# The opening of a fused conformer, attention and MoE kernel: scale's half of the modulation first, the first block's shift as a bias, x's norm with tokens on partitions

## The reference, cut to what matters

```python
def first_block(x, c, ...):
    sc_l = jax.nn.silu(c)                                   # (1, 1024)
    mod_l = (sc_l @ w_mod[i] + b_mod[i])[:, None, :]        # (1, 1, 6144)
    sh1_l, s1_l, g1_l, sh2_l, s2_l, g2_l = jnp.split(mod_l, 6, axis=-1)
    hl = rms_norm(xl, norm1_g[i]) * (1.0 + s1_l) + sh1_l
    yl = conformer_conv(hl, rows, *conv_p)
    xl = xl + g1_l * yl
    ...

def conformer_conv(h, n_seg, w_pw1, b_pw1, w_dw, ...):
    u = h @ w_pw1 + b_pw1                                   # (512, 2048)
    a, gate = jnp.split(u, 2, axis=-1)
    u = a * jax.nn.sigmoid(gate)
    u = dwconv(...)                                         # width 31, in 8 segments of 64 tokens
    ...
```

## Time and profile before

| | |
|---|---|
| Time, median of 3 runs | 2239.32 us (2237.25 to 2240.61) |
| The profiled execution: its own time | 2237.78 us |
| Its span, first to last instruction | 2236.0 us |
| Mean granted TensorE clock | 0.984 |
| Busy: PE, DVE, ACT, POOL | 2166.1 (97%), 989.0 (44%), 396.8 (18%), 69.2 (3%) us |
| First matmul of pw1(0) / first of conv(0) | 36.86 us / 66.80 us from the span's start |

### The profile page before, as it was taken

The page is one execution under the profiler, slowest core; times in us unless marked ns, Lnnn a source line. Parts: engine busy times, 40 slices in busy tenths (PEclk is TensorE's granted clock), DMA queues, the critical chain, the costliest instruction groups (busy, mean ns, idle before and its releaser), DMA issues.

```text
span 2236.0 us, 25125 instructions
## 1 busy us (share of the span) xinstructions
PE 2166.1 (97%) x10252; PEld 1314.6 (59%) x10252; DVE 989.0 (44%) x1435; ACT 396.8 (18%) x783; POOL 69.2 (3%) x89
## 2 busy tenths in 40 slices
PE   7999999999999999998999999999999899999998
PEld 3343488878886777865544444436888544444443
DVE  3883297788855644843122222125555322222222
ACT  3214222002113122842100000002000200000000
POOL 1100100000012000000000000001000000000000
PEclk9999999999999999998999999999999899999999
DMA  9416334577650112032899999996112599999996
GB/s 351 156 44 227 112 131 171 200 252 264 225 207 14 63 39 89 1 151 113 335 428 429 429 427 430 428 425 245 67 76 92 210 423 429 428 428 429 429 428 272
DMA packets 106460, 564.24 MB, mean 252 GB/s; under 512 B 8840, under 2 KB 17550, under 8 KB 78734
## 3 DMA queue, kind: packets, MB, share of 16 engines
q1 hardware_dynamic: 105952, 563.03, 62.6%
q10 hardware_dynamic: 430, 0.13, 0.0%
HBM read 561.04 MB, written 2.10 MB: 252 GB/s over the span
## 4 chain that ended last, share of the span: by engine, by line
PE 84%; DMA 12%; DVE 3%; issue 1%; ACT 1%; SPq 0%; DVEq 0%; ACTq 0%
PE psum L1629 24%; PE psum L2072 16%; PE psum L2058 8%; PE psum L1368 8%; DMA ring<-in_moe_w_down_dram 6%; PE psum L2151 5%; PE psum L1777 4%; PE psum L2108 3%; PE psum L1801 3%; PE psum L1958 2%; PE psum L1934 2%; DMA ring<-in_moe_w_up_dram 2%; PE psum L1909 2%; PE psum L1576 2%; DMA ring<-in_conv_w_pw_dram 1%; DMA ring<-in_mlp_w_dram 1%
## 5 line engine op out<-in xcount | busy, mean ns | idle before, releaser
L2072 PE MATMUL psum<-ring,arena 128*64 128x512 f32 x2048 | 444.8, 593 | 5.8 <-DMA ring<-in_moe_w_up_dram 5.8
L2072 PEld LDWEIGHTS psum<-ring,arena 128*64 128x64 f32 x2048 | 145.0, 137 | 302.3 <-issue 286.0
L2058 PE MATMUL psum<-ring,arena 128*64 128x512 f32 x768 | 224.9, 594 | 2.3 <-DMA ring<-in_moe_w_down_dram 2.0
L2943 DVE TENSOR_TENSOR arena<-psum,arena 128x512 f32<-128x512 f32 x32 | 33.8, 1058 | 410.9 <-PE psum L2072 410.9
L1368 PE MATMUL psum<-hT,ring 128*128 128x512 f32 x416 | 182.1, 597 | 3.7 <-DMA ring<-in_conv_w_pw_dram 3.7
L1629 PE MATMUL psum<-ring 128*128 128x256 f32 x640 | 142.9, 380 | 4.8 <-DVE rstd L2526 4.7
L1368 PEld LDWEIGHTS psum<-hT,ring 128*128 128x128 f32 x416 | 79.3, 192 | 103.2 <-issue 97.7
L1629 PE MATMUL psum<-hT,ring 128*128 128x256 f32 x608 | 138.6, 384 | 0.8 <-ACT hT L891 0.8
L1629 PEld LDWEIGHTS psum<-ring 128*128 128x128 f32 x640 | 121.0, 190 | 24.6 <-issue 8.4
L2108 PEld LDWEIGHTS psum<-arena 128*128 128x128 f32 x1024 | 121.2, 198 | 14.0 <-issue 14.0
L2108 PE MATMUL psum<-arena 128*128 128x128 f32 x1024 | 125.4, 283 | 2.5 <-DVE arena L2970 2.5
(11 more groups left out here) (406 smaller groups left out, 2557.9 us busy)
## 6 DMA issues: line engine op xcount, KB each, us to landing
ring<-in_moe_w_gate_dram SPq DMA_DIRECT2D x64, 2048.0 KB, 19.1
ring<-in_moe_w_up_dram SPq DMA_DIRECT2D x64, 2048.0 KB, 16.4
ring<-in_moe_w_down_dram SPq DMA_DIRECT2D x44, 2048.0 KB, 20.7
ring<-in_ada_w_dram SPq DMA_DIRECT2D x24, 2048.0 KB, 9.0
ring<-in_mlp_w_dram SPq DMA_DIRECT2D x16, 2048.0 KB, 8.6
...
```

Of the source, the lines that this page charges most:

```text
L2058: ins = pe.matmul(psum[64 * e:64 * e + 64, bank + nh, :], src[:, 4 * h + k, 64 * e:64 * e + 64], w[:, k, nh * N:(nh + 1) * N], start=h == ...
L2072: ins = pe.matmul(psum[64 * nh:64 * nh + 64, bank + e, :], src[:, 4 * h + k, 64 * e:64 * e + 64], w[:, k, nh * N:(nh + 1) * N], start=h == ...
```

## The change

Weights. SP's list starts with scale's columns of w_mod alone (`B_SCALE`, two blocks of 4 k by 1024 columns), then pw1's first block, then shift's columns (`B_MOD[0]`, two blocks), then as before. Rows of w_mod are now laid so that partition p holds rows 8p to 8p+7 (`(p k)`), for rounds 0 to 2. `K` moves to ACT's DMA queue, ahead of the vectors, with c loaded once more as `c_own` in the same layout.

Norm. ACT squares `x_tok`, tokens on partitions, with the sum along the row (four 128x1024 instructions), takes the root of 128x4 and DVE the reciprocal of 128x4; four matmuls spread it over the partitions into PSUM (`x_wide`). `norm_stat(NORM1)` and the 128x512 root and reciprocal go.

Modulation. PE multiplies c with scale's first block between x's sixth and seventh tile, with the second after the vectors' turn, copies and turns the rows (`turn_rows(1, ...)`); DVE makes the gain from them and scales x from PSUM's rstd. pw1(0) starts on `hT` without the shift. Then PE multiplies c with shift's half, turns it (`mod_turn(0)`), runs pw1(1)'s first tile, `shift_bias` (the shift times pw1's first block: 16 matmuls of 32x256), pw1(1)'s second tile, and turns the result (`turn_rows(2, ...)`). DVE adds it to b_pw1 as `pw1_bias`, with which ACT takes out the tiles of pw1(0) and pw1(1). ACT adds the shift to `hT` after that, for pw1(2) on.

The rest of the diff renames semaphores and the counts that they reach.

```diff
-        return [add(mods[a][256 * b:256 * b + 256, 2048 * part:2048 * part + 2048].rearrange("(k p) n -> p k n", p=P),
+        return [add(mods[a][:, 2048 * part:2048 * part + 2048].rearrange("(p k) n -> p k n", k=DT)[:, 2 * b:2 * b + 2, :],
                     ("mod_row", rnd + 1)) for b in range(4)]
-    B_MOD = {0: add_mod(0)}
+    B_MOD = {}
+    B_SCALE = [add(mods[0][:, D:2 * D].rearrange("(p k) n -> p k n", k=DT)[:, 4 * b:4 * b + 4, :], ("row_raw", 1))
+               for b in range(2)]
@@ -158,6 +160,9 @@
     for b in range(4):
         B_PW1[b] = add([pw1_rows[:, :, 256 * b + D * (1 - m):256 * b + D * (1 - m) + 256] for m in range(2)],
                        ("tile_done", T_PW1[2 * b + 1] + 2))
+        if b == 0:
+            B_MOD[0] = [add(mods[0][:, 0:D].rearrange("(p k) n -> p k n", k=DT)[:, 4 * m:4 * m + 4, :], ("mod_row", 1))
+                        for m in range(2)]
...
-            squares(NORM1, xT, emptied(T_X))
-            root(NORM1)
+            act.wait_ge(S["x_in"], 32)
+            act.activation(cpad[:, :, 0], c_own[:, :], ACT.Silu).then_inc(S["c_own"], 1)
+            for t in range(NT):
+                ins = act.activation(carve(arena, 6656 + D * t, D), x_tok[:, t, :], ACT.Square,
+                                     accum_out=n_tok[:, 0, t:t + 1])
+            ins.then_inc(S["x_ms"], 1)
+            act.wait_ge(S["x_ms"], 1)
+            act.activation(n_tok[:, 0, :], n_tok[:, 0, :], ACT.Sqrt, scale=1.0 / D, bias=eps[:, 0:1]).then_inc(S["x_rms"], 1)
+            act.wait_ge(S["row_raw"], 1)
+            act.activation(mod_rows[:, :], psum[:, MISC, :], ACT.Copy).then_inc(S["row_sb"], 1)
             act.wait_ge(*emptied(T_V)(0))
-            act.activation(cpad[:, :, 0:3], vecT[:, 0:24].rearrange("p (i k) -> p k i", i=3), ACT.Silu)\
+            act.activation(cpad[:, :, 1:3], vecT[:, 8:24].rearrange("p (i k) -> p k i", i=2), ACT.Silu)\
                 .then_inc(S["c_silu"], 1)
             mod_row(0)
             mod_turned(0)
-            act.wait_ge(S["mod_ready"], 1)
-            shift(NORM1, hT, modv[:, 0, 0:8])
+            act.wait_ge(S["row_raw"], 2)
+            act.activation(mod_rows[:, 0:H], psum[:, STAT, 0:H], ACT.Copy).then_inc(S["row_sb"], 1)
...
                     col = COL["b_pw1"] + (8 if m == 0 else 0) + j
+                    bias = vecT[:, col:col + 1]
+                    if j < 2:
+                        act.wait_ge(S["pw1_bias"], 1)
+                        bias = pw1_bias[:, 2 * m + j:2 * m + j + 1]
                     act.activation(dst[:, j % 2, :], psum[:, t % 6, :], ACT.Sigmoid if m == 0 else ACT.Identity,
-                                   bias=vecT[:, col:col + 1]).then_inc(FREE["act"], 1)
+                                   bias=bias).then_inc(FREE["act"], 1)
+                if m == 0:
+                    act.wait_ge(S["mod_ready"], 1)
+                    shift(NORM1, hT, modv[:, 0, 0:8])
                 conv_out(2 * m)
                 if m == 3:
...
+            def half_gemv(bs):
+
+                for k in range(4 * bs[0], 4 * bs[-1] + 4):
+                    w = arrived(pe, (B_SCALE, B_MOD[0])[len(bs) - 1][k // 4])
+                    for h in range(2):
+                        q = 2 * (k % 2) + h
+                        ins = pe.matmul(psum[32 * q:32 * q + 32, MISC, :], cpad[:, k, :], w[:, k % 4, h * N:(h + 1) * N],
+                                        start=k < 2, stop=k >= DT - 2, skip_group_check=True)
+                return ins
+
+            def turn_rows(n, js):
+
+                pe.wait_ge(S["row_sb"], n)
+                bank = (MISC, STAT)[n - 1]
+                for j in js:
+                    ins = pe.transpose(psum[:, bank, j * P:(j + 1) * P], mod_rows[:, j * P:(j + 1) * P], ident)
+                ins.then_inc(S["row_turned"], 1)
+
+            def shift_bias():
+
+                pe.wait_ge(S["mod_ready"], 1)
+                pe.wait_ge(S["scaled"], DT)
+                w = arrived(pe, B_PW1[0])
+                for k in range(DT):
+                    for m in range(2):
+                        q = 2 * (k % 2) + m
+                        ins = pe.matmul(psum[32 * q:32 * q + 32, STAT, 0:H], modv[:, 0, k:k + 1].to_broadcast([P, 32]),
+                                        w[m][:, k, :], start=k < 2, stop=k >= DT - 2, skip_group_check=True)
+                ins.then_inc(S["row_raw"], 1)
+
             for j in range(DT):
                 turn_tile(T_X + j, [(x_tok[:, t, j * P:(j + 1) * P], P) for t in range(NT)])
-            norm_stat(NORM1)
+                if j == 5:
+                    pe.wait_ge(S["c_own"], 1)
+                    half_gemv((0,))
+            pe.wait_ge(S["x_inv"], 1)
+            for tt in range(NT):
+                ins = pe.matmul(psum[:, STAT, tt * P:(tt + 1) * P], n_tok[:, 1, tt:tt + 1].to_broadcast([P, P]), ident,
+                                start=True, stop=True, skip_group_check=True)
+            ins.then_inc(S["x_wide"], 1)
             pe.wait_ge(S["vec_in"], 16 * N_VEC)
             turn_tile(T_V, [(vec_rows[0:VEC_ROWS[g], g, :], VEC_ROWS[g]) for g in (0, 1)])
-            mod_gemv(0)
-            mod_turn(0)
-
-            def pw1(j):
+            half_gemv((1,)).then_inc(S["row_raw"], 1)
+            turn_rows(1, range(4))
...
+            def pw1(j, ms=(0, 1)):
                 w = arrived(pe, B_PW1[j // 2])
-                for m in range(2):
+                for m in ms:
                     t = T_PW1[j] + m
                     begin(t)
-                    dense(t, w[m], (j % 2) * P, lambda k: hT[:, k, :], DT,
-                          ready=("h_ready", 0) if j == 0 and m == 0 else None).then_inc(S["tile_done"], 1)
+                    ready = ("scaled" if j == 0 else "h_ready", 0) if j in (0, 2) and m == 0 else None
+                    dense(t, w[m], (j % 2) * P, lambda k: hT[:, k, :], DT, ready=ready).then_inc(S["tile_done"], 1)
...
             for m in range(4):
                 pw1(2 * m)
                 if m == 0:
+                    pe.wait_ge(S["c_silu"], 1)
+                    pe.wait_ge(S["gains"], 1)
+                    half_gemv((0, 1)).then_inc(S["mod_row"], 1)
                     pe.wait_ge(S["taps_in"], 16 * N_TAPS)
                     pe.wait_ge(S["tap_pad"], 1)
                     turn_tile(T_TAPS, [(vec_rows[0:VEC_ROWS[g], g, :], VEC_ROWS[g]) for g in range(2, 6)])
+                    mod_turn(0)
+                    pw1(1, (0,))
+                    shift_bias()
+                    pw1(1, (1,))
+                    turn_rows(2, range(2))
                 if m == 2:
-                    pe.wait_ge(S["rms_ready"], 1)
+                    pe.wait_ge(S["pw1_bias"], 1)
                 if m >= 2:
                     conv_mean(2 * m - 3)
-                pw1(2 * m + 1)
+                if m:
+                    pw1(2 * m + 1)
                 conv(2 * m)
...
+            dve.wait_ge(S["x_rms"], 1)
+            dve.reciprocal(n_tok[:, 1, :], n_tok[:, 0, :]).then_inc(S["x_inv"], 1)
...
-            scale(NORM1, xT, hT, gain[:, 0, :], made=1)
+            dve.wait_ge(S["row_turned"], 1)
+            part = psum[:, MISC, :].rearrange("p (j b h c) -> p b h j c", j=4, b=2, h=2)[:, :, :, :, 0]
+            scale_v = modv[:, 0, 8:16].rearrange("p (h j) -> p h j", h=2)
+            link(dve.tensor_tensor(scale_v, part[:, 0], vec("b_mod0", 8).rearrange("p (h j) -> p h j", h=2), ALU.add))
+            link(dve.tensor_tensor(scale_v, scale_v, part[:, 1], ALU.add))
+            dve.scalar_tensor_tensor(out=gain[:, 0, :], in0=modv[:, 0, 8:16], scalar=one[:, 0:1], in1=vec("norm1_g"),
+                                     op0=ALU.add, op1=ALU.mult).then_inc(S["gains"], 1)
+            dve.wait_ge(S["gains"], 1)
+            dve.wait_ge(S["x_wide"], 1)
+            for j in range(DT):
+                dve.scalar_tensor_tensor(out=hT[:, j, :], in0=xT[:, j, :], scalar=gain[:, 0, j:j + 1], in1=psum[:, STAT, :],
+                                         op0=ALU.mult, op1=ALU.mult).then_inc(S["scaled"], 1)
...
+            dve.wait_ge(S["row_turned"], 2)
+            b_pw1 = vecT[:, COL["b_pw1"]:COL["b_pw1"] + 16].rearrange("p (m k) -> p m k", m=2)
+            part = psum[:, STAT, 0:H].rearrange("p (j b m c) -> p b m j c", j=2, b=2, m=2)[:, :, :, :, 0]
+            for m in range(2):
+                own = pw1_bias[:, 2 * m:2 * m + 2]
+                link(dve.tensor_tensor(own, part[:, 0, m], b_pw1[:, 1 - m, 0:2], ALU.add))
+                ins = dve.tensor_tensor(own, own, part[:, 1, m], ALU.add)
+            ins.then_inc(S["pw1_bias"], 1)
```

58 lines of the change are left out of this document (30 added, 28 removed).

## The result

| | before | after |
|---|---|---|
| Time, median (lowest to highest), 6 runs each, side by side | 2239.11 us (2236.5 to 2240.61) | 2248.61 us (2245.76 to 2252.04) |
| Ratio after to before, 95% interval | | 1.0044 (1.0034 to 1.0054) |
| The profiled execution: its own time, its span, mean clock | 2237.78, 2236.0 us, 0.984 | 2247.34, 2245.6 us, 0.983 |

The change makes the kernel slower, by 9.5 us between the medians.

A forecast was written before the change was run, and what follows sets the result against it. PE bounds the kernel, through pw1(0)'s start and the work between pw1(0) and conv(0). -10.1 - 1.6 + 6.5 + 10.7 + 1.6 = +7.1 us on the median of 2239.3 gives 2246.4 us; range 2242.0 to 2251.

The forecast's parts named there:

- Start, -10.1: pw1(0)'s weights queue behind 4.19 MB of w_mod instead of 8.39, so it starts at 26.8 instead of 36.86 us.
- Clock at the start, -1.6: PE's clock holds after 3.4 us idle, so pw1(0) takes 13.9 us instead of 15.52; bounds 0 and -1.6.
- half clock as before: Rival at pw1(0): the start stays at half clock, the -1.6 goes, +8.7 us, 2248.0; chance 0.33.
- Added on PE, +6.5: Between pw1(0) and conv(0): shift's half 3.5, its turn 0.9, shift_bias 1.8, two transposes 0.3 us.
- Wait, 10.7: PE waits before conv(0): additions 0.9, table load 1.3, two tiles 1.3, glu and spread 7.2 us.
- Half clock in conv(0), +1.6: After the long idle time conv(0) starts at half clock, losing 1.6 us; bounds 0.2 and 2.
- every later stage shifted by the same amount: Sign after conv(0): the shift of conv(0), starting at 71 to 73.5 us, reaches all later stages unchanged.
- The slow layout: Rival for w_mod's transfers: new row layout runs at half of 417 GB/s, +17 us, 2256; chance 0.07.
- The drain of 1.38 us beside a table's load: On ACT's path to conv(0): a drain per table switch would add 1.4 us; left out, as the trace shows none.

The follow-up runs named there:

- e6: Changed kernel with the old order of loading, both blocks of shift's weights ahead of pw1's first block again; 2259.15 us.
- e8: Kernel before with only the new norm of x, tokens on partitions; 2241.37 us, ratio 1.0017 to the kernel before.
- e11: Changed kernel once more, unchanged, for a second profile; 2255.48 us in a single execution.
- e5: Changed kernel, first two tiles without the shift's bias, DVE's additions behind glu(0), ACT's row copy behind spread(0); 2233.06 us.
- e1: Changed kernel with the two transposes of shift_bias's result moved ahead of pw1(1)'s second tile; 2239.92 us.
- e4: Changed kernel with ACT's wait for pw1_bias written before the wait for the tile, so the table loads earlier; 2248.1 us.
- e2: Changed kernel with shift_bias and its two transposes moved ahead of both tiles of pw1(1); 2235.92 us.
- e3: Changed kernel with ACT taking out pw1(0)'s and pw1(1)'s tiles with b_pw1 alone, not waiting for pw1_bias; 2244.68 us.
- e10: Changed kernel with matmuls nobody reads filling PE's waits, 4 ahead of pw1(0) and 14 at conv(0)'s head; 2242.7 us.
- e7: Changed kernel with shift_bias and transposes ahead of both pw1(1) tiles, plus four matmuls nobody reads ahead of pw1(0); 2233.03 us.
- e9: Changed kernel, start filled with matmuls nobody reads, shift_bias and transposes between the matmuls of pw1(1)'s first tile; 2234.6 us.
- e12: Kernel before with five matmuls nobody reads filling PE's wait ahead of pw1(0); 2236.84 us, ratio 0.9996.

## Why the prediction was right

Direction, range and mechanism held: 2246.4 us was forecast, 2248.61 measured (range 2242 to 2251). From profile to profile +7.1 was forecast and +9.6 measured; most of the difference is in a place that the sum did not have, the LayerNorm's statistics. By its own steps:

- **Start, -10.1.** Measured -10.36. That the queue's order alone gives it, e6 shows; that the new norm is hidden, the rows show: the first scaled slice's instruction starts at 24.89 and is done at about 25.6 (eight take 5.36), 0.9 us before the weights. It had been forecast for 24.8, 2 us before them; the margin was half of that. e8 shows that the norm alone is no gain and, in the old order, a loss.
- **Clock at the start, -1.6, against half clock as before.** -1.52 in the first profile, but 16.95 us in e11. The step treated as a property of the kernel what differs from one execution to the next: forecast and rival were both seen. That the first profile agrees with the -1.6 is luck, and the measured median lies nearer to the rival's 2248.0 than to the forecast. Seven profiles have this wait unfilled, at about 2.5 us: in the first of the changed kernel and in e5 the clock held (14.00 us), in e1 to e4 and e11 it did not (15.69 to 16.99). A chance of 0.33 for the rival was too low.
- **Added on PE, +6.5.** Measured 6.51; `shift_bias` 1.93, by its columns, not by its instructions (3.5).
- **Wait, 10.7.** Measured 10.76, link by link: additions with their hand-overs 0.8 (0.9 taken), table 1.3, tiles 1.3, glu and spread 7.2. e1, e2 and e5 show that it is the loss, and e4 that the table's load stands inside it. The prediction took the place of the two transposes for what lets the wait stand. That holds for 6.9 of the 10.8 us: e1 moves nothing else and leaves 3.88, and the wait went only when `shift_bias` moved too (e2). What it didn't say is that the bias holds three entries in the queues (e3). And it took from the load at 11.73 that a table's load stands on the wait ahead of it; the load at 40.59, in the same rows, had not stood on `tile_done`. It came out right because there were two waits here (e4).
- **Half clock in conv(0), +1.6.** Measured 2.05 (2.50 in e11), a little above its upper bound of 2; e10 shows it to be a cost by itself, and that conv(2)'s small margin takes 0.3 of it, the reason that the lower bound gave. The stretch from 275 to 282 that the bound leaned on was not beside sparse work: PE is busy for 5.88 of 6.90 us there.
- **Not in the sum: +1.5 in the LayerNorm's statistics.** The step that failed is "every later stage shifted by the same amount". PEclk fell there in the changed kernel, e1, e3, e4, e6, e7 and e9 to e12 (9.18 to 9.37 us), and not in the kernel before, e2, e5 and e8 (7.67 or 7.68). What decides it stays open: the wait ahead is 2.16 or 2.17 us in all of them, and e12, which is the kernel before but for its filled wait, had the fall too. Perhaps the kernel before has it in other executions; then it is no part of the change's cost.
- **The slow layout.** 398 and 408 GB/s: no loss. The Trainium skill, "DMA: Bandwidth & Descriptors", section "Latency and other measured facts", has a loss for row steps of large powers of two (164 GB/s at 2 MiB and 103 at 4 MiB, where 4 MiB with 4 KiB more gave the full 214); 192 KB is no such step, and no run here tests the rule.
- **The drain of 1.38 us beside a table's load**, which the Trainium skill, "ScalarE: Activation LUTs", section "What ACT_TABLE_LOAD costs", adds, was left out, rightly: at 62.25 the load takes 1.28 us and the tile starts at 63.54. With the drain the wait would have been 12.1.
